# Forgetting attention of block 2 by head pairs, beside the state-space projections

## What is computed

```python
def forgetting_attention(q, k, v, f_logit, f_bias, norm_g):
    ...
    log_f = jax.nn.log_sigmoid(f_logit.astype(f32) + f_bias.astype(f32))
    cum = jnp.cumsum(log_f, axis=1).transpose(0, 2, 1)
    ...
    def block(args):
        qi, ci, i = args
        s = jnp.einsum('bhqd,bhkd->bhqk', qi, kh).astype(f32) * scale
        s = s + ci[..., :, None] - cum[:, :, None, :]
        q_pos = i * ATTN_BLOCK + jnp.arange(ATTN_BLOCK)
        s = jnp.where(k_pos[None, :] <= q_pos[:, None], s, -jnp.inf)
        p = jax.nn.softmax(s, axis=-1)
        return jnp.einsum('bhqk,bhkd->bhqd', p.astype(vh.dtype), vh)
    ...
    return rms_norm_2(o, norm_g)

def ssd_mixer(z, xbc, dt_raw, conv_w, conv_b, dt_bias, a_log, d_skip, norm_g):
    ...
    xbc = jax.nn.silu(causal_depthwise_conv(xbc, conv_w, conv_b))
    ...
    y = y * jax.nn.silu(z.astype(f32)).reshape(bsz, seq, SSD_GROUPS, r * SSD_HEAD_DIM)
```

## Time and profile before

| | us |
|---|---|
| median of 3 runs | 1522.38 (1517.9 to 1522.44) |
| profiled execution | 1521.11 |
| its span on the engines | 1519.4 |
| TensorE busy | 1321.9 (87%) |
| VectorE busy | 592.7 (39%) |
| ScalarE busy | 347.4 (23%) |
| `xbc` projections start | 683.1 |
| Fox norm's sums start | 802.8 |
| out projection of block 2 starts | 857.7 |

### The profile page before, as it was taken

The page is one execution under the profiler, slowest core; times in us unless marked ns, Lnnn a source line. Parts: engine busy times, 40 slices in busy tenths (PEclk is TensorE's granted clock), DMA queues, the critical chain, the costliest instruction groups (busy, mean ns, idle before and its releaser), DMA issues.

```text
span 1519.4 us, 21160 instructions
## 1 busy us (share of the span) xinstructions
PE 1321.9 (87%) x7554; PEld 659.6 (43%) x7555; DVE 592.7 (39%) x1109; ACT 347.4 (23%) x741; POOL 170.2 (11%) x276
## 2 busy tenths in 40 slices
PE   4989999998999999999779995788888888888891
PEld 1445656568744444464354454333233333333330
DVE  1466373744123333496675735122122211221214
ACT  1222232321244422212353421001101011011012
POOL 3011111111110000000000000111111111111102
PEclk8999999999999999999799996799999999899896
DMA  9252707061271100223100484369999999899974
GB/s 325 96 195 48 246 17 269 9 195 31 65 213 44 42 1 0 74 70 83 42 1 0 149 349 180 114 221 394 400 404 407 410 403 404 352 404 402 406 308 185
DMA packets 112864, 302.38 MB, mean 199 GB/s; under 512 B 10778, under 2 KB 67250, under 8 KB 91792
## 3 DMA queue, kind: packets, MB, share of 16 engines
q1 hardware_dynamic: 103488, 285.12, 50.3%
q0 software_dynamic: 9296, 16.17, 3.6%
HBM read 297.75 MB, written 13.73 MB: 205 GB/s over the span
## 4 chain that ended last, share of the span: by engine, by line
PE 77%; DVE 9%; DMA 6%; issue 3%; DVEq 2%; ACT 2%; POOL 1%; SPq 0%; POOLq 0%; ACTq 0%; PEldq 0%
PE bank L814 22%; PE bank L2672 17%; PE bank L2688 8%; PE bank L745 7%; PE bank L860 4%; PE bank L823 3%; DMA arena<-in_w_ada 2%; PE bank L803 2%; DVE hT L2766 1%; DVE hT L2764 1%; DMA yT<-xn_scratch,idx_col 1%; DMA arena<-in_ada_w 1%; DVEq L2525 1%; DMA expert_rows<-cactB,place_col 1%; PE bank L1042 1%
## 5 line engine op out<-in xcount | busy, mean ns | idle before, releaser
L814 PE MATMUL bank<-hT,arena 128*128 128x512 f32 x768 | 339.4, 599 | 0.0
L2672 PE MATMUL bank<-arena,hT 128*64 128x512 f32 x1024 | 257.4, 661 | 55.3 <-DVE hT L2766 55.3
L814 PEld LDWEIGHTS bank<-hT,arena 128*128 128x128 f32 x768 | 144.7, 191 | 180.1 <-issue 177.3
L2672 PEld LDWEIGHTS bank<-arena,hT 128*64 128x64 f32 x1024 | 78.4, 152 | 213.8 <-issue 168.1
L745 PE MATMUL bank<-arena,yT 128*128 128x512 f32 x256 | 114.5, 602 | 2.3 <-DVE yT L1615 2.3
L2772 DVE TENSOR_SCALAR hT<-hT 128x256 f32<-128x256 f32 x32 | 9.4, 294 | 273.2 <-ACT hT L2731 273.2
L2688 PE MATMUL bank<-arena,yT 128*64 128x512 f32 x512 | 115.4, 592 | 0.6 <-ACT yT L2739 0.6
L2731 ACT ACTIVATE hT<-bank 128x256 f32<-128x256 f32 x32 | 12.3, 384 | 327.0 <-PE bank L2672 327.0
L745 PEld LDWEIGHTS bank<-arena,yT 128*128 128x128 f32 x256 | 48.2, 192 | 60.6 <-issue 56.3
L860 PEld LDWEIGHTS bank<-arena 64*64 64x64 f32 x1856 | 59.5, 135 | 28.4 <-issue 14.4
L860 PE MATMUL bank<-arena 64*64 64x64 f32 x1856 | 64.1, 220 | 7.0 <-POOLq L655 4.5
(11 more groups left out here) (452 smaller groups left out, 1577.7 us busy)
## 6 DMA issues: line engine op xcount, KB each, us to landing
arena<-in_w_gate SPq DMA_DIRECT2D x64, 1024.0 KB, 17.4
arena<-in_w_up SPq DMA_DIRECT2D x64, 1024.0 KB, 21.4
arena<-in_w_down SPq DMA_DIRECT2D x32, 2048.0 KB, 18.9
arena<-in_w_in SPq DMA_DIRECT2D x55, 512.0 KB, 4.4
arena<-in_ada_w SPq DMA_DIRECT2D x24, 1024.0 KB, 5.3
arena<-in_w_ada SPq DMA_DIRECT2D x8, 1024.0 KB, 12.8
arena<-in_w_out SPq DMA_DIRECT2D x8, 1024.0 KB, 14.0
arena<-in_w_ada SPq DMA_DIRECT2D x8, 512.0 KB, 5.0
```

Of the source, the lines that this page charges most:

```text
L814: last = T.matmul(bank[0:rows, :], w[:, k, 0:rows], hT[:, k, :], start=k == 0, stop=k == KD - 1)
L2672: last = T.matmul(banks[1 + ub][MT * h:MT * h + MT, :], tile.xT[:, k, :], wgu[u][:, :, k, 256 * h:256 * h + 256], start=k == 0, stop=k == ...
```

## The change

Fox runs by pairs of heads: 8 steps `(g, t)` in place of 16. Queries and keys of the two heads lie in partitions 0 to 63 and 64 to 127 and are multiplied in two row tiles of the array, each into its own bank; outputs of both heads go to the two column halves of one bank. Queries are scaled by the negative factor, so scores are negated and the row maximum becomes a minimum: one VectorE instruction adds the key decay and finds it. The query's own decay is left out. The causal mask is added by TensorE, as an identity product into the open bank. The `xbc` projections, which stood ahead of Fox, now stand one in each step, and VectorE's short convolutions follow one step behind. Turned tokens, C-B products and turned B move behind Fox, the first z projection goes between them, and each of the other z projections moves one place ahead.

```diff
@@ plan @@
-        for i in range(8):
-            plan(("xbc", i), "act")
         for h in range(4):
             plan(("cumk", h), "dve")
         plan(("alast",), "dve")
-        for i in range(AHEAD):
-            plan(("fs", i), "dve")
...
+        plan_fox_scores(0)
+        for i in range(len(STEPS_F)):
+            if i + 1 < len(STEPS_F):
+                plan_fox_scores(i + 1)
+            plan(("xbc", i), "act")
+            for h in range(2):
+                plan(("fPT", i, h), "act")
             if i:
                 plan(("fO", i - 1), "act")
@@ pe_block2 @@
-            for i in range(8):
-                pe_proj(("xbc", i))
             for h in range(4):
                 full(T.matmul(fill(("cumk", h))[:, :], sel[:, 8 + h, :], AC12, start=True, stop=True))
...
-            def score(i):
-                h, t = divmod(i, TT)
+            def scores(i):
+
+                g, t = STEPS_F[i]
                 n = (t + 1) * P
-                full(T.matmul(fill(("fs", i))[:, 0:n], fq[:, h, CH(t)], fk[:, h // 2, 0:n], start=True, stop=True))
+                two = [fill(("fs", i, h), h) for h in range(2)]
+                for h in range(2):
+                    r = slice(64 * h, 64 * h + 64)
+                    T.matmul(two[h][:, 0:n], fq[r, g, CH(t)], fk[r, g, 0:n], start=True, stop=False)
+                for h in range(2):
+                    full(T.matmul(two[h][:, CH(t)], ident[:, :], causal, start=False, stop=True))
...
+            scores(0)
+            for i in range(len(STEPS_F)):
+                if i + 1 < len(STEPS_F):
+                    scores(i + 1)
+                pe_proj(("xbc", i))
+                turn_probs(i)
                 if i:
                     out_rows(i - 1)
-            out_rows(4 * TT - 1)
+            out_rows(len(STEPS_F) - 1)
+            eng.wait_ge(s_xc, 4)
+            for n in range(TT):
+                bank = fill(("xtok", n))
...
+            pe_proj(("z", 0))
+            eng.wait_ge(s_xc, 8)
+            for n in range(2):
+                bank = fill(("cb", n))
...
@@ act_block2 @@
+            for i in range(len(STEPS_F)):
+                n = (STEPS_F[i][1] + 1) * P
+                if i + 1 < len(STEPS_F):
                     probs_exp(i + 1)
...
+                xbc_in(i)
+                for h in range(2):
+                    copy_out(("fPT", i, h), fpt[:, 2 * (i % 2) + h, 0:n], lambda bank: bank[:, 0:n])
                 if i:
                     out_rows(i - 1)
+                    xbc_exp(i - 1)
+                if i > 1:
+                    xbc_sigmoid(i - 2)
@@ dve_block2 @@
+            def scores(i):
+
+                g, t = STEPS_F[i]
                 n = (t + 1) * P
...
+                for h in range(2):
+                    u = 2 * (i % 2) + h
+                    name = ("fs", i, h)
+                    bank = take(V, name)
+                    empty(V, "dve", V.tensor_tensor_reduce(
+                        out=fsc[:, u, 0:n], in0=bank[:, 0:n], in1=cumk[:, 2 * g + h, 0:n], scale=1.0,
+                        scalar=3.0e38, op0=ADD, op1=MIN, accum_out=fnmx[:, u:u + 1]), name)
+                    eng.sem_inc(s_fmx, 1)
...
+            scores(0)
+            for i in range(len(STEPS_F)):
+                if i + 1 < len(STEPS_F):
+                    scores(i + 1)
+                probs(i)
+                if i:
+                    x_conv(i - 1)
+                if i > 1:
+                    x_clamp(eng, i - 2)
+                if i > 2:
+                    x_silu(eng, i - 3)
```

258 lines of the change are left out of this document (119 added, 139 removed).

## The result

| | device time, median | lowest to highest | ratio to before, 95% interval | profiled execution (span) |
|---|---|---|---|---|
| before | 1522.41 us (4 runs) | 1517.9 to 1524.87 | 1 | 1521.11 us (1519.4) |
| changed | 1502.26 us (4 runs) | 1499.55 to 1504.71 | 0.985 [0.9818, 0.9883] | 1499.55 us (1497.8) |

What follows compares the result with a forecast made beforehand. TensorE was taken to bound block 2. A gain of 23.1 - 2.1 - 1.2 = 19.8 us took the profiled 1521.1 to 1501.3; half of the median's 1.3 us excess added gave 1502, range 1495 to 1511.

Steps and rivals of the forecast that it cites:

- What bounds the stretch: Block 2, 683.1 to 802.8 us: TensorE's own sequence counts; it holds 77% of the chain that ended last.
- First wait: Second pair of scores: TensorE waits 4.9 us, to 692.9, for VectorE to empty the first decay row's bank.
- Clock behind the wait: Behind TensorE's first wait: a lowered clock costs 2.1 us, with 0 and 3.4 as the ends.
- Eight steps: Fox's steps with projections, scores, masks, turning and outputs: 73.5 us of TensorE work, nothing waited for.
- After the steps: Last outputs, tokens, z, C-B products, turned B: 1.9 + 1.8 + 6.9 + 1.8 + 0.9 us, no wait.
- The sum: From 683.1 to the Fox norm's sums: 96.6 us against 119.7, a gain of 23.1, less 2.1 for the clock.
- The tail: Fox norm to out projection: z's leaving gains nothing; two TensorE waits of some 4 us; clock costs 1.2.
- rival D: Fox norm to out projection: TensorE sets the tail, z's leaving gives up to 6.9 us more, 1495; chance 0.07.
- Behind the block: After the out projection: expert weight loads start from the same events, shifted, so the gain passes on in full.
- rival B: In the eight steps: engines hand over too late, 4 to 12 us go, 1506 to 1514 us; chance 0.22.
- Rival C: Fox scores and outputs: tiles don't run beside each other, 4.3 + 4.3 us more, 1510.6; chance 0.05.
- The rule on tiling modes: In the steps: mode changes drain TensorE, but block 1's rows carry that cost, so the sum stays.

Runs made afterwards that it cites:

- e5: Changed kernel with the causal mask left out of Fox's scores; 1495.94 us, ratio 0.9823.
- e6: Changed kernel with VectorE's combined score instruction issued twice per head and step; 1507.41 us, ratio 0.9902.
- e2: Changed kernel with the four decay-row banks emptied by ScalarE in place of VectorE; 1497.26 us, ratio 0.9816.
- e9: e2 with the four decay-row products replaced by equally long products over 128 partitions (values differ); one profiled execution, 1492.2 us.
- e10: e2 with small transposes moved earlier and one decay row behind each of the four query and key projections; 1492.81 us, ratio 0.9786.
- e3: Changed kernel with the z projections back in their old places, none ahead of the C-B products; 1499.98 us, ratio 0.9839.
- e12: The changed kernel again, unedited, as a control; 1500.76 us, ratio 0.9828.
- e4: Changed kernel with the two heads' outputs written one head after the other, not alternating; 1505.01 us, ratio 0.9873.
- e1: Changed kernel with all eight xbc projections and short convolutions ahead of Fox again; 1531.09 us, ratio 1.0031.
- e11: e10 with the mask added by GpSimd and each xbc projection one step earlier; 1495.31 us, ratio 0.9789.
- e7: e2 with the decay rows of heads 2 and 3 moved behind the second xbc projection; 1496.98 us, ratio 0.9844.
- e8: e7 with the mask added to the key decays by GpSimd, without TensorE's mask products; 1495.29 us, ratio 0.9826.

## Why the prediction was right

*What bounds the stretch.* Right, and shown: taking the mask off TensorE shortens it by 3.0 of the 4.3 us that it costs on the path, and the other 1.3 are found in TensorE's projections (e5); 6.8 us more of VectorE work doesn't lengthen it (e6).

*First wait.* Forecast 4.9 us to 692.9, measured 4.32 to 693.43. The mechanism (the bank of the first decay row, emptied behind the taps) is the one in the row.

*Clock behind the wait.* Forecast 2.1, measured 2.3 (second scores 1.16 instead of 0.63, mask 1.01 instead of 0.55, first projection 8.15 instead of 6.87, from start to start). **The size was right and the cause was wrong, so the agreement is luck.** The prediction read it from rows in which a wait stood ahead. In the changed kernel the clock had fallen before the wait: it stood at 0.98 from 686 to 688, and the mask at 687.89, in front of the wait, is slow already. e2 has no wait and loses 3.2 us in the four pieces from its first mask on, e9 and e10 lose nothing. The kernel before says the same in the rows ahead of its wait of 10.6 us, which starts at 744.3, behind its own four decay rows (738.19 to 741.8). TensorE is busy throughout, and the clock is at 1.00 before 742, at 0.70 in the mean of this row, and at 0.50 behind it:

```profile
742.00:744.00 2.00, 2.00 (x8) 1.08 (x8) 1.12 (x2) 0.43 (x1) 0.00 (x0) 0.70 0.00 0
```

A wait can do it as well: behind 6.11 us of it the clock is down in e3. No run has the wait of 4.3 us without the decay rows in front of it, so what that wait would have cost by itself isn't known.

*Eight steps.* Forecast 73.5. From 693.43 to 769.81, less 2.3 for the clock, are 74.1. Projections, scores (0.84 and 1.06 for 3 and 4 blocks) and turning (0.31 for 1) came as taken from block 1's rows. The one term that was off is the mask: 0.55 a pair, not 0.45, since the row it was taken from, four C-B products between full-array products (762.69), has no change of tiles beside it. Seven times 0.1 is the difference.

*After the steps.* Forecast 1.9 + 1.8 + 6.9 + 1.8 + 0.9 = 13.3; measured 769.81 to 782.55 = 12.7. z hides VectorE's end with 0.7 us to spare, where I had counted 1.4, and e3 shows what it hides: a wait of 6.1 us.

*The sum.* From the decay rows to the sums 99.04, forecast 98.7.

*The tail.* Forecast: no gain from z's leaving, waits of 4 and 4 us, 1.2 for the clock. Measured 54.71 us against 54.90 before, with waits of 4.29 and 2.83: z's leaving gave nothing, as argued from the earlier trace rows, and rival D is out. The clock's 1.2 wasn't paid in this execution, but it was in others: from the sums to the out projection e10 took 54.6 and e5 54.7, e2 56.0 and e12 56.1, with the same work and the last state outputs (L2052 in the changed kernel) at 0.68 or at 1.15. e3 and e4 took 55.1 there and then 8.40 and 8.44 for the first 16 instructions of the out projection, which take 7.13 elsewhere. So this term is a coin of some 1.4 us, not a constant, and the profiled execution had the lucky side.

*Behind the block.* 661.7 us before and 660.5 after, from the out projection to the end of the span: the gain was passed on. The 1.2 us between them say nothing: without e6 these times lie between 656 and 663 us in all profiles.

*What was priced wrong without harm.* VectorE was to be 80% busy between 692 and 768; it was 60% (44.36 of the 74 us from 692 to 766). 7.3 us in a step of 9.1 to 9.8 was the longest step, taken for all eight. So rival B had more chance than it deserved. Rival C's sign was a scores pair of 4 blocks above 1.9 us; it took 1.13 (713.22). Its price for the outputs, 4.3 us, is 1.2 for the order that e4 has. And the prediction didn't ask what the pairs bring alone: nothing (e1, without any work beside them). All of the 20 us come with the projections that now stand where TensorE waited.

*The rule on tiling modes.* The Trainium skill (TensorEngine Tiling (Array Packing), Key Properties) says that a change of tiling mode drains TensorE. e5 agrees in sign: the projection that follows 64-partition scores directly takes 0.10 us more than the one that follows a full-array mask. The mask's 0.55 instead of 0.45 is the same 0.10 at the other place. In eight steps that is under 1 us.

## What to carry to other kernels

Putting independent dense work between a producer and the consumer that waits for its result pays more than making the small pieces of that chain smaller: here the same Fox in pairs gained nothing with no work beside it and 20 us beside the projections. Price such a step from start to start in a stage that has the same form already, and price what stands between unlike tiles by a row where tiles change. When taking more work off one engine, look first at what the second hangs on: VectorE's slack of 0.7 us stayed while 3 and 6 us came off the stretch (e5, e10), since its end moved with the last projection, and was gone when the projections stood a step earlier (e11).

## What the runs showed of the hardware

- The granted clock fell from 1.00 to 0.50 without any idle time of TensorE (e2, 2.00 of 2.00 us busy in both rows, 1.00 and then 0.60 in the mean, 1.22 for a mask; the kernel before, busy for 2.00 of 2.00 us with 0.70 in the mean), behind four products over 12 partitions; with products of the same length over 128 partitions at that place it stayed at 1.00 (e9), and also with the narrow ones set one by one between projections of 7 us (e10). With two of them together it fell in one place and not in the other, both in e7 and in e8. The Trainium skill (TensorE: Matmul & The Clock Gate, Part 1: The HAM clock gate) has the clock set by how busy TensorE has been; by the profile's busy time e2 speaks against that, so a product's busy time can't be all that counts.
- Where it falls varies between executions of the same kernel: behind the decay rows (3.67 us long, at full speed) in the changed kernel, inside them (5.46) in e12, the same kernel again.
- Column tiles of two heads run beside each other for the most part even when one head's products all come first: 1.58 us against 1.09 for 16 instructions.
